# Neighbourhood attention on one core: the product with the values turned round, two tiles side by side in the array

## What is computed

```python
s_win = einsum('brchd,brkwhd->bhrckw', qg, kb) * scale + bias   # 8 rows of keys around the query's row
s_win = where(col_ok, s_win, -inf)                              # 16 columns around its column
s_ctx = einsum('brchd,bshd->bhrcs', qg, ck) * scale             # 256 cached context keys
p = softmax(concatenate([s_win, s_ctx]))
o = einsum(p_win, vb) + einsum(p_ctx, cv)
y_a = o * silu(z_a)
...
m = g_a * (y_a @ w_proj_a) + g_b * (y_b @ w_proj_b)
out = rmsnorm(x + gate * (m @ w_out))
```

## Time and profile before

| | us |
|---|---|
| median of 3 runs | 1938.49 |
| the profiled execution, its own time | 1937.24 |
| its span, first to last instruction | 1935.5 |
| TensorE busy in the span | 1900.1 (98%) |
| VectorE busy | 1021.9 (53%) |
| ScalarE busy | 535.2 (28%) |
| GpSimd busy | 124.8 (6%) |
| granted TensorE clock, share of full speed | 0.998 |

### The profile page before, as it was taken

One profiled execution on the slowest core, in us unless ns is written; L12 is line 12 of the kernel. 1 busy time (PEld: TensorE's weight loads), 2 busy tenths in 40 slices (PEclk: granted clock), 3 DMA queues, 4 the chain that ended last, 5 costly groups with the idle time before them and its releaser, 6 DMA issues.

```text
span 1935.5 us, 26939 instructions
## 1 busy us (share of the span) xinstructions
PE 1900.1 (98%) x10707; PEld 1632.8 (84%) x10707; DVE 1021.9 (53%) x1617; ACT 535.2 (28%) x1109; POOL 124.8 (6%) x225
## 2 busy tenths in 40 slices
PE   7999999999999999999999999999999899999998
PEld 1788899988888888888888889999999888878886
DVE  2544412111288258718835875657567655554444
ACT  2641101011111111111111115565657322221221
POOL 0000000000000000000000032222420000000000
PEclk9999999999999999999999999999999999999999
DMA  8614413233022112202211268786764666483421
GB/s 277 195 63 162 154 66 128 66 131 109 28 79 75 43 55 72 78 20 89 77 57 40 75 152 199 147 187 123 170 159 110 223 204 196 154 270 119 153 99 55
DMA packets 205944, 235.06 MB, mean 121 GB/s; under 512 B 46347, under 2 KB 154747, under 8 KB 201723
## 3 DMA queue, kind: packets, MB, share of 16 engines
q1 hardware_dynamic: 205560, 233.23, 40.6%
q10 hardware_dynamic: 259, 0.11, 0.0%
HBM read 152.52 MB, written 80.78 MB: 121 GB/s over the span
## 4 chain that ended last, share of the span: by engine, by line
PE 92%; DMA 2%; DVE 2%; ACT 2%; SPq 1%; issue 1%; POOL 0%; POOLq 0%; ACTq 0%; DVEq 0%
PE banks L759 17%; PE banks L760 17%; PE banks L761 17%; PE banks L1125 5%; PE banks L1650 3%; PE banks L1648 3%; PE banks L1649 3%; PE banks L1127 3%; PE banks L1618 3%; PE banks L1620 3%; PE banks L1619 3%; PE banks L1103 2%; PE banks L754 2%; PE banks L756 2%; PE banks L755 2%; PE banks L1108 2%
## 5 line engine op out<-in xcount | busy, mean ns | idle before, releaser
L759 PE MATMUL banks<-h_hi,w_hi 128*128 128x512 f32 (+1 forms) x1600 | 592.7, 370 | 2.5 <-DVE w_lo L544 1.5
L761 PE MATMUL banks<-h_hi,w_lo 128*128 128x512 f32 (+1 forms) x1600 | 588.9, 368 | 0.0
L760 PE MATMUL banks<-h_lo,w_hi 128*128 128x512 f32 (+1 forms) x1600 | 588.9, 368 | 0.0
L700 DVE SCALAR_TENSOR_TENSOR conv_acc<-glu_out,taps,conv_acc 128x773 f32<-128x773 f32 x360 | 371.6, 1032 | 12.3
L759 PEld LDWEIGHTS banks<-h_hi,w_hi 128*128 128x128 f32 x1600 | 301.7, 189 | 56.0 <-issue 2.6
L761 PEld LDWEIGHTS banks<-h_hi,w_lo 128*128 128x128 f32 x1600 | 301.5, 188 | 50.5
L760 PEld LDWEIGHTS banks<-h_lo,w_hi 128*128 128x128 f32 x1600 | 301.8, 189 | 49.0
L484 ACT ACTIVATE out_stage<-banks,param_cols 128x512 f32<-128x512 f32 (+1 forms) x120 | 77.0, 647 | 442.4 <-PE banks L761 436.5
L1160 DVE CUSTOM_DVE_ANT_0 scores<-banks,bias 128x640 f32<-128x640 f32 (+2 forms) x128 | 106.3, 831 | 58.4 <-PE banks L1089 57.8
L1618 PE MATMUL banks<-y_hi,wp_hi 128*128 128x512 f32 (+1 forms) x320 | 121.7, 380 | 1.2 <-DVE y_lo L1788 0.6
L1620 PE MATMUL banks<-y_hi,wp_lo 128*128 128x512 f32 (+1 forms) x320 | 119.5, 373 | 0.0
(11 more groups left out here) (157 smaller groups left out, 2485.2 us busy)
## 6 DMA issues: line engine op xcount, KB each, us to landing
proj<-out_stage SPq DMA_DIRECT2D x96, 256.0 KB, 2.0
w_raw<-in_w_in SPq DMA_DIRECT2D x44, 512.0 KB, 4.0
gates_in<-proj SPq DMA_DIRECT2D x64, 256.0 KB, 3.1
k_hi<-k_hi_rows SPq DMA_DIRECT2D x16, 640.0 KB, 12.9
k_lo<-k_lo_rows SPq DMA_DIRECT2D x16, 640.0 KB, 15.3
w_ada<-in_w_ada SPq DMA_DIRECT2D x8, 1024.0 KB, 11.2
x_rows<-in_x_sample SPq DMA_DIRECT2D x4, 2048.0 KB, 11.3
x_out<-in_x_sample SPq DMA_DIRECT2D x16, 512.0 KB, 3.5
```

The costliest lines, as they stand in the source:

```text
L700: op = dve.scalar_tensor_tensor(dst, src, tap, dst, ALU.mult, ALU.add)
L759: pe.matmul(out, w_hi[:, s, k], h_hi[c][:, k], start=first, stop=False)
L760: pe.matmul(out, w_hi[:, s, k], h_lo[c][:, k], start=False, stop=False)
L761: op = pe.matmul(out, w_lo[:, s, k], h_hi[c][:, k], start=False, stop=last)
```

## The change

The product with the values is turned round: the values are the weights (up to 128 keys by 64 channels), and the 128 columns of `probs_t` are streamed. The output lies channel by token, 64 partitions high. Two tiles of the same head are taken together (`PAIRS`: the same tile column, two neighbouring bands), one in the array's columns 0 to 63, the other in columns 64 to 127, and their outputs lie in partitions 0 to 63 and 64 to 127 of bank 2. The matmuls of the two tiles alternate.

The sum of the exponents comes from ScalarE's accumulator (`accum_out`). Since the output has channels on partitions, the inverse sums must be turned instead: `invert` makes a reciprocal 128 columns wide (each of two sums repeated 64 times), TensorE turns it into bank 2, and `gate_out` multiplies z_a by it (L1211 of the new file) and then the output by that (L1213). `copy_out`, `norm_out` and `turn_out` are gone, the ones columns too; `probs_t` has four buffers instead of two; the last window block is turned beside the context blocks, so `copy_rest` is one instruction. z_a and y lie in halves of 64 partitions, loaded and stored in three parts each per head.

Cut to what matters (a `...` line marks what is left out):

```diff
-    ps_o, ps_y = banks[:, 2], banks[:, 3]
+    ps_o, ps_inv = banks[:, 2, 0:P], banks[:, 2, P:2 * P]
...
+    PAIRS = [(8 * e + b, 8 * e + 4 + b) for e in range(2) for b in range(4)] + [(LT, LT + 1)]
+    PPH = len(PAIRS)
+    TILES = [i for pair in PAIRS for i in pair]
+    BODY = [(m // TPH, TILES[m % TPH]) for m in range(NT)]
...
-        def weigh_values(m):
-            n, i = BODY[m]
-            u = n % 2
-            if i == 0:
-                pe.wait_ge(v_in[u], 288 * (n // 2 + 1))
-            if m in (0, TPH):
-                pe.wait_ge(ones_set, 2 * n + 2)
-            pe.wait_ge(pt_act, m + 1)
-            pe.wait_ge(pt_dve, m + 1)
-            if m:
-                pe.wait_ge(o_done, m)
-            nb, w4 = key_blocks(i)
-            out = ps_o[:, 0:DH + 1]
-            for j in range(nb):
-                pe.matmul(out, pT[0:w4, m % 2, j], v_win[u][0:w4, i % 4, BANDS[i // 4][0] // 4 + j], start=(j == 0), stop=False)
...
+        def weigh_values(k):
+            m = 2 * k
+            n = BODY[m][0]
+            if m % TPH == 0:
+                pe.wait_ge(v_in[n % 2], 288 * (n // 2 + 1))
+            pe.wait_ge(inv_done, k + 1)
+            if k:
+                pe.wait_ge(y_done, k)
+            pe.transpose(ps_inv, inv[:, k % 2].rearrange("p e d -> p (e d)"), cst.ident[:])
+            pe.wait_ge(pt_act, m + 2)
+            pe.wait_ge(pt_dve, m + 2)
+            both = [values_of(m), values_of(m + 1)]
+            for j in range(max(len(b) for b in both)):
+                for e in range(2):
+                    if j < len(both[e]):
+                        rows, slot, v = both[e][j]
+                        last = j == len(both[e]) - 1
+                        op = pe.matmul(ps_o[DH * e:DH * e + DH], v, pT[0:rows, (m + e) % 4, slot], start=(j == 0), stop=last)
+                        if last:
+                            op.then_inc(pv_done, 1)
...
-            if 1 <= m <= NT:
-                weigh_values(m - 1)
-            if m - 3 in group_end:
-                turn_out(pe, group_end[m - 3])
+            if m >= 2 and m % 2 == 0:
+                weigh_values(m // 2 - 1)
...
+        def invert(k):
+            dve.wait_ge(exp_done, 2 * k + 2)
+            if k >= 2:
+                dve.wait_ge(pv_done, 2 * (k - 1))
+            at = 2 * k % 4
+            dve.reciprocal(inv[:, k % 2], sums[:, at:at + 2].unsqueeze(2).to_broadcast([P, 2, DH])).then_inc(inv_done, 1)
...
+            dve.tensor_tensor(scaled, i_t, z, ALU.mult).then_inc(z_scaled, 1)
+            dve.wait_ge(z_scaled, k + 1)
+            dve.tensor_tensor(y, o, scaled, ALU.mult).then_inc(y_done, 1)
...
             if m < NT:
                 copy_window(m)
+                if m % 2:
+                    invert(m // 2)
             if m + 2 < NT:
                 soften(m + 2)
...
+            if m >= 3 and m % 2:
+                gate_out(m // 2 - 1)
...
-            act.activation(p_sb[:, m % 2, 0:nk + CTX], src, ACT.Exp, bias=stat[:, m % 4, 0:1], scale=-1.0).then_inc(exp_done, 1)
+            act.activation(p_sb[:, m % 2, 0:nk + CTX], src, ACT.Exp, bias=stat[:, m % 4, 0:1], scale=-1.0,
+                           accum_out=sums[:, m % 4:m % 4 + 1]).then_inc(exp_done, 1)
```

More of the change, by code:

```diff
@@ L947, in wait_bank @@
             pe.wait_ge(exp_done, NT)
-        elif bank >= 2:
-            pe.wait_ge(o_done, NT)
+        elif bank == 3:
+            pe.wait_ge(tail_stage.lin_done, 4)
+        elif bank == 2:
+            pe.wait_ge(y_done, PPH * HEADS)
         else:
@@ L952, in wait_bank, with y_rows, store_y @@
             pe.wait_ge(pt_act, NT)
-        if bank == 3:
-            pe.wait_ge(y_done, TPH * HEADS // 2)
-    Y_PARTS = [(0, 512, 4), (512, 512, 8), (1024, 512, 12), (1536, 768, 18)]
-    Y_STORES = 16 * (HEADS // 2 - 1 + len(Y_PARTS))
-    def store_last(sp, part):
-        at, w, tiles = Y_PARTS[part]
-        sp.wait_ge(y_done, TPH * (HEADS // 2 - 1) + tiles)
-        sp.dma_start(io.ya[P * (HEADS // 2 - 1):P * HEADS // 2, at:at + w], y_sb[:, at:at + w]).then_inc(y_out, 16)
+    Y_PARTS = [([0], 4), ([1], 8), ([2], 9)]
+    def y_rows(n, half, part):
+        rows = slice(DH * n, DH * n + DH)
+        if part == 2:
+            return rows, slice(LAT + P * half, LAT + P * half + P), slice(LAT // 2, LAT // 2 + P)
+        at = LAT // 2 * part + 512 * half
+        return rows, slice(at, at + 512), slice(512 * part, 512 * part + 512)
+    def store_y(sp, n, part):
+        sp.wait_ge(y_done, PPH * n + Y_PARTS[part][1])
+        for half in range(2):
+            rows, tok, at = y_rows(n, half, part)
+            sp.dma_start(io.ya[rows, tok], y_sb[DH * half:DH * half + DH, n % 2, at]).then_inc(y_out[n % 2], 16)
     def store_last_y(sp):
-        store_last(sp, 3)
+        store_y(sp, HEADS - 1, 2)
     def wait_y_stored(sp):
-        sp.wait_ge(y_out, Y_STORES)
-    io.wait_bank, io.store_last_y, io.wait_y_stored, io.y_done = wait_bank, store_last_y, wait_y_stored, y_done
-    io.last_turn = lambda pe: turn_out(pe, HEADS // 2 * GROUPS - 1)
+        for u in range(2):
+            sp.wait_ge(y_out[u], 96 * HEADS // 2)
+    io.wait_bank, io.store_last_y, io.wait_y_stored = wait_bank, store_last_y, wait_y_stored
     tail_stage = tail(nc, io, cst)
@@ L1022, in load_first, with load_z @@
                 q.dma_start(cmask[:], io.col_mask.rearrange("t p r -> p t r")).then_inc(mask_in, 16)
-        def load_z(hp):
-            sp.wait_ge(y_done, TPH * hp)
-            sp.dma_start(z_sb[:], io.proj[ZA0 + P * hp:ZA0 + P * hp + P]).then_inc(z_in, 16)
-        def store_y(hp):
-            sp.wait_ge(y_done, TPH * (hp + 1))
-            sp.dma_start(io.ya[P * hp:P * hp + P], y_sb[:]).then_inc(y_out, 16)
+        def load_z(n):
+            if n >= 2:
+                sp.wait_ge(y_done, PPH * (n - 1))
+            for half in range(2):
+                for part in range(3):
+                    rows, tok, at = y_rows(n, half, part)
+                    src = io.proj[ZA0:ZA0 + WA][rows, tok]
+                    sp.dma_start(z_sb[DH * half:DH * half + DH, n % 2, at], src).then_inc(z_in[n % 2], 16)
         front_sync(sp, load_first)
@@ L1043, in _ @@
             load_v(n)
-            if n % 2:
-                store_y(n // 2 - 1)
-                load_z(n // 2)
+            for part in range(3):
+                store_y(sp, n - 2, part)
+            load_z(n)
         for done in (s_mm, pv_done, red):
@@ L1050, in _ @@
         tail_stage.load_wp(sp)
-        store_last(sp, 0)
-        sp.wait_ge(y_out, 16 * HEADS // 2)
+        for part in range(3):
+            store_y(sp, HEADS - 2, part)
+        store_y(sp, HEADS - 1, 0)
+        sp.wait_ge(y_out[0], 96 * HEADS // 2)
+        sp.wait_ge(y_out[1], 96 * (HEADS // 2 - 1) + 32)
         tail_stage.load_ya(sp, 0)
-        store_last(sp, 1)
-        store_last(sp, 2)
+        store_y(sp, HEADS - 1, 1)
         for done in (s_mm, pv_done, red, exp_done):
@@ L1058, in _ @@
         tail_stage.sync(sp)
-    def turn_out(pe, gg):
-        pe.wait_ge(normed, gg + 1)
-        pe.wait_ge(y_done, NG * gg)
-        if gg in (GROUPS, 2 * GROUPS):
-            pe.wait_ge(tail_stage.lin_done, 2 * gg // GROUPS)
-        for t in range(NG):
-            tr = pe.transpose(ps_y[:, P * t:P * t + P], o_norm[:, gg % 2, t], cst.ident[:])
-        tr.then_inc(y_turned, 1)
     @block.tensor
@@ L1126, in weigh_values @@
-            for j in range(2):
-                mm = pe.matmul(out, pT[:, m % 2, 4 + j], v_ctx[u][:, (2 if i >= LT else 0) + j], start=(nb == 0 and j == 0),
-                               stop=(j == 1))
-            mm.then_inc(pv_done, 1)
+            nb, w4 = key_blocks(i)
+            win = [(w4, j if j < nb - 1 else 3, v_win[n % 2][0:w4, i % 4, BANDS[i // 4][0] // 4 + j]) for j in range(nb)]
+            return win + [(P, 4 + j, v_ctx[n % 2][:, (2 if i >= LT else 0) + j]) for j in range(2)]
```

130 lines of the change are left out of this document (48 added, 82 removed).

## The result

| | time, us | ratio to before, 95% interval |
|---|---|---|
| before, 4 runs | 1938.78 (1935.69 to 1939.55) | |
| changed, 4 runs | 1980.51 (1978.27 to 1981.82) | 1.0217 [1.0199, 1.0235] |

A forecast was written before the change was run, and what follows sets the result against it. TensorE, busy 98%, was taken to bound the kernel. A new TensorE-VectorE ring makes the stage 319 against 326, with 3 us for the tail: 1937.2 - 4 = 1933; the reciprocal's 27 gives 1960, range 1930 to 2025.

The forecast's parts named there:

- the rival of the dearer reciprocal: Wide reciprocal on VectorE takes 1.20 us, 0.68 late, 44 us, with the halves overlapping: 1977; chance 0.10.
- the ring: Once per pair, TensorE's product waits for VectorE's gating, which stands behind a softening needing TensorE's scores; 4.65 us per latent pair.
- part 1: Product with the values on TensorE: array halves overlap, so a latent pair takes 1.40 us, a context pair 0.50.
- the serial rival: Halves run one after the other, products 2.42 and 0.88 us, 68 us more: 2001 or 2028; chance 0.19.
- half an overlap: Loads pulled ahead by one pass only: 0.082 per pass, product 1.81 us, 26 us more: 1960 or 1987; chance 0.14.
- part 2: Entering and leaving the array halves on TensorE: 0.147 us per change, two per pair, 21 us.
- part 4: 128-column reciprocal on VectorE ahead of the odd softening: 0.94 us, 0.42 late, 27 us.
- SP issues more and smaller loads of z and stores of y, all a head ahead of use: Hidden parts, SP's issue of z loads and y stores: claimed to be early enough; no time added.
- the likeliest case: Halves overlap and the reciprocal takes 0.94 us: 1960, own range 1948 to 1968; chance 0.30.
- the steps' sum: Attention stage before the change, 128 latent steps of 2.43 us and 16 context steps of 0.91: 326 us.
- the tail's pieces: Projection-weight splits and norms in VectorE's order, hidden before, now lengthen its waits by part of their length: 3 us.
- By this alone the change would win 42: TensorE's own work per latent pair falls from 4.86 to 4.20 us: 0.66 x 64 = 42 us.

The follow-up runs named there:

- gate_only: Changed kernel with only the gating of a pair moved one step earlier on VectorE, z still loaded late; 1947.62 us, ratio 1.0050.
- z_gate: z_first with the gating of a pair one step earlier, behind the even step's softening; 1927.07 us, ratio 0.9948.
- z_first: Changed kernel with the first head's z loaded ahead of the second head's window, keys and values; 1950.93 us, ratio 1.0074.
- z_serial: z_first with the two tiles' product matmuls not alternating, all of the first tile, then the second; 1994.92 us, ratio 1.0301.
- z_gate_serial_switch: z_gate with the product tile by tile and the turn of the inverse sums between the two tiles' passes; 1997.46 us, ratio 1.0307.
- z_narrow: z_first with the reciprocal of the two sums alone, then a broad copy to 128 columns; 1933.31 us, ratio 0.9977.
- z_gate_order: z_gate with each bias window issued behind the previous head's values, and y stores and z loads ahead of the values; 1913.47 us, ratio 0.9871.

## Why the prediction was right or wrong

The measured 1980.5 lies in the range, but that is luck. The range went up to 2025 for the case in which the halves don't overlap, and they do. Of the distance to before, 28 us of the stage come from a wait that the prediction had put at nothing, and without it the forecast would have been 9 us too high. By the number alone one would have taken the rival of the dearer reciprocal (1977), which the rows exclude.

**Right: the ring and what waits.** 0.54 us each, 68 times, for the gating, where 0.4 to 1 was written down. Taking the gating out of the ring brought 33 us (gate_only against the changed kernel) and 24 us (z_gate against z_first).

**Right: the halves overlap (part 1).** A latent pair's product is twelve slots of 0.109: 1.31 (1.40 was forecast with 12.5 slots of 0.112). The product's 1.46 us excludes the serial rival (2.42) and half an overlap (1.81), and z_serial shows what losing half of the overlap costs. What the Trainium skill says of independent tiles (TensorEngine Tiling (Array Packing), Key Properties) now has a row: starts 0.007 us apart. The trace agrees.

**Right in size, a little too much in the sum: mode changes (part 2).** 0.147 each was forecast, and z_gate_serial_switch pays 0.29 for two more. In the ring of the changed kernel the turn takes 0.23 to the product's start, where 0.165 + 0.147 = 0.31 was in the sum, and the product with its first load and its leaving 1.46, where 1.40 + 0.147 = 1.55 was. So the product's way from turn to next transposes is 0.23 + 1.46 = 1.69 us, not 1.86. Against this stands the latency from the gating's end to TensorE's start, 0.146 in all 71 places, where 0.05 was estimated.

**Right: the reciprocal (part 4).** 0.942 us (72 of them), 0.94 forecast; 0.86 to the next instruction, 0.86 forecast; the softening 0.44 late, 0.42 forecast. z_narrow takes 26 us out of the periods, 27 forecast. The estimate that the prediction worked out from the Trainium skill (VectorE: DVE Perf Modes, the walkthrough of the 8-slice pipeline), 1.07 us beside a fixed part, is above the whole measured time.

**Wrong: "SP issues more and smaller loads of z and stores of y, all a head ahead of use".** This is the step that failed. The first head's z is issued behind the second head's loads and is needed 20 us before; the step counted instructions and never held the issue's time (1196.82 in the trace of before) against the new time of first use. VectorE waited 25.5 us, TensorE behind it came back to half of its clock for 5 us (2 us more), and z_first gives 29.6. Without this the kernel takes 1950.9, inside the likeliest case's own range of 1948 to 1968.

**Mis-sized: what the ring hides of the stage of before.** The ring over the stage was forecast at 319 + 27 = 346; the periods of undisturbed heads sum to 8 x 43.35 = 347. But from the first transposes to the last product the records show 337.5 us in before, where the steps' sum had 326, and 352.7 in z_first, where it had 349 (346 and 3 for the tail's pieces). So the stage got 15 longer, not 23, and those 8 us are most of the distance between 1960 and 1951. Of the 337.5, 4.5 are the tail's transposes, which TensorE, then without waits, paid in full; the other 7 are left over, by subtraction: steps longer than the mean that I built from two tiles. That the ring hides such pieces is argued from this, not shown by a run. In the changed kernel the stage is 380.7: 28 by z and 15 by the ring make 43, and the rest of the kernel got 2 shorter.

**"By this alone the change would win 42"** was reached by half: with the gating early and the loads in order (z_gate_order) the stage is 315.9 us, 21.6 less than before. Most of what is missing to 42 stands in the rows of that kernel:

```profile
1391.09 0.28 PE L1091 MATMUL banks<-k_lo,q_split 128*128 128x256 f32 x1
1391.54 0.50 PE L1105 MATMUL banks<-ident,probs 128*96 128x128 f32 x3 [0.17 <-ACT probs_t L1254]
```

```profile
1390.90 0.49 ACT L1254 ACTIVATE probs_t<-banks 128x384 f32<-128x384 f32 x1 [0.41 <-PE banks L1110]
```

The product stands behind the even step's scores, so the next even step's transposes have only scores between them and the odd step's. They start 0.15 us behind ScalarE's copy of the odd step (1391.39), and 0.45 behind the start of the last scores, where the turn of the inverse sums follows such scores after 0.12. The old order had a product between any two steps' transposes. Over the stage 63 such transposes start 0.14 to 0.16 us behind that copy, 0.24 late in the median and 18 us in all. That this copy is the cause is read from the order of these rows and the latency; no run took it away. z_first has the same delay (66 places, 20 us), and the 4.20 us of TensorE's own work in the prediction had no term for it.

## What to carry to other kernels

When a change makes a buffer's first use earlier, put the new time of use beside the time at which its load is issued in the trace of before, for the first round above all: that one line was worth 29.6 of the 42 us. When TensorE's work shrinks and the next operation waits for a result that an in-order engine makes behind other work, move that result's instructions ahead before making them shorter: the early gating gave 24 to 33 us and left at most about 4 of the long reciprocal's 27. And when single periods get long after a gain, look at the queue of issues next: two changes of order there gave another 14 us.

## What was not expected of the hardware

- The weight loads of two column halves run side by side too. A load of 64 columns has a record of 0.137 us, and the records of the two halves start 0.007 apart, as the passes do:

```profile
1342.60 0.14 PEld L1136 LDWEIGHTS banks<-probs_t,v_ctx 128*64 128x64 f32 x1
1342.60 0.14 PEld L1136 LDWEIGHTS banks<-probs_t,v_win 128*64 128x64 f32 x1
```

- Passes of the second half start ahead of three passes of the first that were issued earlier (z_serial, 0.930 us into the product, where the first half's last three start at 1.04 to 1.25), so a short product of four passes per half needs no alternating order: 0.595 us tile by tile, 0.588 in turns.
- A reciprocal costs far more by its width than other operations of VectorE: 0.153 us for 2 columns, 0.187 for 6, 0.942 for 128, thus about 0.0063 per column; the broad copy of 128 columns takes 0.23, and a product of two tiles 0.28 for 128 columns and 0.56 for 384, thus 0.0011 per column.
- The stall of TensorE cost more than its length. In the changed kernel TensorE stood from 1176.5 us to 1202.9 and its granted clock was 0.50 from 1180.8 to 1208.1, so it worked at half speed after the wait: 2 us on top of it. gate_only shows the same (0.50 from 1179.0 to 1209.7), and z_first, without the wait, has 1.00 throughout that stretch.
- Sixteen issues of the values' strided loads hold SyncE's queue for 15 to 24 us of a head of 38 to 43 us. With window, q, k, z and y the queue has no rest in the first heads, so their order decides which load is late. Whether the queue is the next bound is not shown: in z_gate_order it rests for 5.6 us from 1350.8 and for 5.9 us from 1389.2, and no period there is above 5.0 us.
